# A closing norm's factor gets a place of its own, and two queries' swaps go ahead of a weight load

## The reference, cut to what matters

```python
x = first_block(x, ...)                       # ends: return _rmsnorm(x, final_norm_w)
x = second_block(x, ...)

def hybrid_layer(x, c_silu, cos, sin, norm_g, ...):
    u = rms_norm(x, norm_g) * (1 + scale) + shift
    z = u @ w_in                              # aq ak av ag iq ik iw bq bk bv bg cq ck cv cg ma mb mc
    # a: for each query the 128 best keys by an index score, attention over them
    #    score = sum over 4 heads of iw * relu(rope(iq) @ rope(ik)); top_k(score)
    # b: window attention with sinks;  c: stick-breaking attention
    merged = sigmoid(ma) * (ya @ w_br_a) + sigmoid(mb) * (yb @ w_br_b) + sigmoid(mc) * (yc @ w_br_c)
    return x + gate * (merged @ w_out)
```

## Time and profile before

| what | value |
|---|---|
| median of 3 runs | 2800.11 us (2791.91 to 2801.91) |
| the profiled execution's own time | 2794.37 us |
| its span | 2792.6 us |
| TensorE busy | 2681.3 us (96%) |
| VectorE busy | 1816.1 us (65%) |
| ScalarE busy | 1152.6 us (41%) |
| mean granted clock of TensorE | 0.981 |

### The profile page before, as it was taken

The page is one execution under the profiler, slowest core; times in us unless marked ns, Lnnn a source line. Parts: engine busy times, 40 slices in busy tenths (PEclk is TensorE's granted clock), DMA queues, the critical chain, the costliest instruction groups (busy, mean ns, idle before and its releaser), DMA issues.

```text
span 2792.6 us, 36953 instructions
## 1 busy us (share of the span) xinstructions
PE 2681.3 (96%) x14886; PEld 2154.3 (77%) x14886; DVE 1816.1 (65%) x2968; ACT 1152.6 (41%) x1900; POOL 693.0 (25%) x514
## 2 busy tenths in 40 slices
PE   6999899999999998999999999998999999999997
PEld 5877578888878676888887878776787788777776
DVE  7789668867577775877557768744546548544534
ACT  3243544323242454433224464344434455444432
POOL 0000047988700004356540032000100122000100
PEclk9999999999999998999999999999999999999999
DMA  8453034554432112344432535231223222322312
GB/s 273 122 144 104 29 121 151 166 166 159 147 119 57 59 59 83 121 143 150 139 123 85 163 94 159 85 106 33 91 64 106 85 73 80 91 76 72 96 61 78
DMA packets 281114, 302.59 MB, mean 108 GB/s; under 512 B 9968, under 2 KB 263024, under 8 KB 280944
## 3 DMA queue, kind: packets, MB, share of 16 engines
q1 hardware_dynamic: 267568, 250.21, 28.8%
q0 software_dynamic: 13088, 49.55, 5.4%
q10 hardware_dynamic: 288, 0.47, 0.1%
HBM read 289.97 MB, written 2.10 MB: 105 GB/s over the span
## 4 chain that ended last, share of the span: by engine, by line
PE 86%; DVE 7%; ACT 4%; DMA 1%; issue 1%; SPq 0%; POOL 0%; DVEq 0%; ACTq 0%
PE ps L568 84%; PE ps L776 2%; DVE wl L1410 1%; DVE hl L1416 1%; DVE adaacc L1416 1%; DMA raw<-in_w_in 1%; ACT wh L934 0%; DVE recat L1708 0%; ACT recat L934 0%; ACT hh L934 0%; DMA stage<-in_w_ada 0%; DVE rawt L1416 0%; DMA t1s<-rawt 0%; ACT att_p L934 0%; DVE ca L1416 0%
## 5 line engine op out<-in xcount | busy, mean ns | idle before, releaser
L568 PE MATMUL ps<-hh,wh 128*128 128x512 f32 x2208 | 891.8, 404 | 24.1 <-DVE wl L1410 10.2
L568 PE MATMUL ps<-hh,wl 128*128 128x512 f32 x2208 | 866.8, 393 | 0.0
L568 PE MATMUL ps<-hl,wh 128*128 128x512 f32 x2208 | 865.5, 392 | 0.0
L1410 DVE TENSOR_TENSOR wl<-raw,wh 128x2048 fp32r<-128x2048 f32 (+3 forms) x234 | 500.9, 2149 | 167.7 <-ACT wh L934 167.5
L568 PEld LDWEIGHTS ps<-hh,wh 128*128 128x128 f32 x2208 | 416.5, 189 | 140.8 <-issue 40.4
L568 PEld LDWEIGHTS ps<-hh,wl 128*128 128x128 f32 x2208 | 416.4, 189 | 92.4
L568 PEld LDWEIGHTS ps<-hl,wh 128*128 128x128 f32 x2208 | 417.3, 189 | 80.2
L934 ACT ACTIVATE wh<-raw 128x2048 fp32r<-128x2048 f32 (+3 forms) x234 | 370.0, 1591 | 205.8 <-PE ps L568 191.4
L568 PE MATMUL ps<-fh,wh 128*128 128x512 f32 x432 | 171.6, 397 | 0.0
L568 PE MATMUL ps<-fh,wl 128*128 128x512 f32 x432 | 168.3, 390 | 0.0
L568 PE MATMUL ps<-fl,wh 128*128 128x512 f32 x432 | 168.2, 389 | 0.0
(11 more groups left out here) (298 smaller groups left out, 4136.5 us busy)
## 6 DMA issues: line engine op xcount, KB each, us to landing
raw<-in_w_in SPq DMA_DIRECT2D x75, 1024.0 KB, 5.3
raw<-in_w_up SPq DMA_DIRECT2D x46, 1024.0 KB, 5.1
strewn<-in_w_ada POOLq DMA_DIRECT2D x80, 512.0 KB, 4.1
raw<-in_w_ada SPq DMA_DIRECT2D x24, 1024.0 KB, 5.3
raw<-in_w_in SPq DMA_DIRECT2D x44, 512.0 KB, 5.1
raw<-in_w_out SPq DMA_DIRECT2D x16, 1024.0 KB, 5.1
raw<-in_w_down SPq DMA_DIRECT2D x16, 1024.0 KB, 5.2
stage<-in_w_ada SPq DMA_DIRECT2D x8, 1024.0 KB, 11.6
```

Of the source, the lines that this page charges most:

```text
L568: return e.matmul(o, a, b, start=start, stop=stop, skip_group_check=True)
L1410: return e.tensor_tensor(o, a, b, op)
```

## The change

Two things. First, SyncE doesn't issue the load behind the split of the first cq chunk at once in the second stack's layers: it issues the eight swaps of iq first and the load behind them. Second, the factor of the first stack's closing norm goes to `M.fin_rr`, the last quarter of `M.bq`. The index ReLU of layer 0 then waits for the factor only, the eight scalings stand one behind each tile of the values c ("v2"), they have a cost in the planner's table, and the rotation of queries b on GpSimd waits for the last of them.

```diff
@@ Memory
         self.bq = sb("bq", [128, 4, 512])
+        self.fin_rr = self.bq[:, 3, :]
@@ COST
-    "bv": (("ACT", 0.6, True),), "bvt": (("PE", 0.5, True), ("ACT", 0.6, True)), "iw": (("PE", 0.5, True), ("DVE", 0.2, True)),
+    "final": (("DVE", 0.75, True),), "bv": (("ACT", 0.6, True),), "bvt": (("PE", 0.5, True), ("ACT", 0.6, True)), "iw": (("PE", 0.5, True), ("DVE", 0.2, True)),
@@ scalar_program, inv_rms
         if tag == ("fin", 0):
-            rr = M.nrm[:, 0, :]
+            rr = M.fin_rr
@@ scalar_program, index_scores
-        go.wait_ge(*(at("weighed", *before) if before else at("hl", ("m3", 1), KD - 1) if l else at("xf", ("m3", 0), KD - 1)))
+        go.wait_ge(*(at("weighed", *before) if before else at("hl", ("m3", 1), KD - 1) if l else at("rr", ("fin", 0))))
@@ vector_program, final
-        rr = M.nrm[:, 0, :] if w == "fin" else M.rr[:, :]
+        rr = M.fin_rr if w == "fin" else M.rr[:, :]
@@ gpsimd_program, rope
+        if nm == "bq" and l == 0:
+            go.wait_ge(*at("xf", ("m3", 0), KD - 1))
@@ sync_program
-    for kind, *rest_ in X.order:
+    for n, (kind, *rest_) in enumerate(X.order):
         if kind == "rope":
             rope(*rest_[:3])
         elif kind in ("split", "ada", "adap"):
             free.add(rest_[-1])
+        if kind == "split" and X.order[n + 1][:1] == ("em",) and X.order[n + 1][1][0] == "m3":
+            continue
+        if kind in ("split", "ada", "adap") or kind == "rope" and rest_[1:3] == ["iq", 1]:
             while loads and loads[0][1]["raw_before"] in free:
                 load(*loads.pop(0))
@@ order_block2
-    finals = [("final", ("fin", 0), "fin", k, k + 2) for k in range(0, KD, 2)] if l == 0 else []
+    finals = [("final", ("fin", 0), "fin", k, k + 1) for k in range(KD)] if l == 0 else []
@@ order_block2, main
-        if finals:
+        if finals and units[0][0] == "v2":
             mains.append(([finals.pop(0)], 1, False, None))
@@ order_block2
-    index, last = [], [("final", ("fin", 0), "fin", 6, 8)] if l == 0 else []
+    index, last = [], []
```

## The result

| | before | after |
|---|---|---|
| median of 20 runs each | 2798.22 us (2787.97 to 2806.32) | 2784.32 us (2779.76 to 2800.38) |
| the profiled execution's own time | 2794.37 us | 2782.49 us |
| its span | 2792.6 us | 2780.7 us |
| first query tile of layer 0 to that of layer 1 | 653.3 us | 643.1 us |
| from there to the end | 621.4 us | 617.1 us |

The ratio is 0.9959, 95% interval 0.995 to 0.9968: some 11 us (the two medians lie 13.9 us apart), under the bound of 0.5% that the prediction set. A later series of the same program gave 0.9969 (0.9955 to 0.9982). By the profiles layer 0 gained 10.2 us and layer 1 4.2; the first stack, which the change doesn't touch, took 2.5 us more in the execution after. Between executions it varies more than that: the first query tile starts anywhere from 1517.7 to 1531.8 us in the profiles of this study.

What follows compares the result with a forecast made beforehand. TensorE bounds the kernel (86% of the chain), so a change pays only where it waits or runs slowly. Layer 0's 9.7 plus layer 1's 1.1 us make 10.8; median forecast 2789 us, range 2776 to 2800, the forecast's own 2784 to 2795.

Steps and rivals of the forecast that it cites:

- The swaps' part, the wait removed: Second query tile: swaps ahead of the load land in 2.2 us, removing waits of 3.64 (layer 0) and 2.39 us.
- The late load: Layer 0 key tile: load issued behind eight swaps lands 5.3 us later; 1.4 us of new waiting for the residue.
- sum of 8.1 us: Whole change: estimated gain in place of 10.8 us if each load counted with 5.3 lands 0.85 us later.
- The closing factor: Layer 0 index ReLU: the 2.12 us wait goes, a new 2.5 us wait comes; layer 0 gives 9.7 us in all.
- Layer 1: Start of layer 1: only the swaps' order acts; 1.1 us stays, the rest handed on to the weights' chain.
- The planner: Layer 0 top-k steps: scalings' cost (6 us) and scores about 6 us earlier about cancel; nothing, 3 us either way.
- the rival in which the tail grows: Layer 0 attention a: scalings planned ahead of top-k steps end them later; 2801 us if the tail doubled; chance 0.11.
- my own sign of being wrong: Wrong if attention a's or b's tail changes by over 10 us, value tiles miss residues, or swaps still take 5 us.
- The cover of the scalings: Value tiles of layer 0: VectorE, busy 28.62 of 37.00 us, fits 5.5 us more, so it costs nothing.
- The load is too late: Both layers: swaps ahead give nothing as swaps stay late or weights set the pace; 2795 us; chance 0.16.
- part 1: SyncE's queue in both layers: index query swaps go ahead of the load; 3.64 us wait removed in layer 0.
- The tail goes away: Layer 0 attention a: top-k steps end a stage earlier and it spreads over matmul tiles; 2778 us; chance 0.17.

Runs made afterwards that it cites:

- e1: Kernel before with the index queries' swaps ahead of the load in both layers, nothing else; ratio to before 0.9981 (0.9968 to 0.9993).
- e4: Kernel before with the factor in its own place and the ReLU waiting for it alone; scalings and planner as before; ratio 0.9982 (0.9971 to 0.9994).
- e5: Kernel before with swaps ahead of the load and the factor in its own place; scalings unmoved, without planner cost; ratio 0.9953 (0.9938 to 0.9968).
- e2: Kernel before with the swaps ahead of the load in layer 1 only; ratio to before 0.9988 (0.9976 to 1.0).
- e12: The changed kernel unaltered, for a second profile; ratio to before 0.9969 (0.9955 to 0.9982), layer 0 645.6 us.
- e9: Changed kernel without the scalings' planner cost, two unread matmuls added before each TensorE wait in layer 0's last six attention a blocks; median 2780.77 us.

## Why the prediction was right, and where it was not

The median came to 2784.32 us where 2789 was forecast, at the lower edge of the forecast's own range of 2784 to 2795. By the profiles the two layers gave 14.4 us where 10.8 were forecast. The size is in part luck: layer 1 gave 3.1 us more than its term, two shifts of the planner met near nothing for another reason than the one given, and the clock at the start of layer 0 differs by up to 3.4 us of time (by the half) between profiles of the same start.

*The swaps' part, the wait removed.* Right: 3.64 and 2.39 us became 0.45 and none. e1 shows it alone, with 3.2 and 4.3 us. The fourth swap took 3.76 us, between the 2.2 that I took and the bound of 5.8. That the 5.76 us of before were all due to the load ahead of it was too simple: in layer 1, behind the same load, the fourth swap took 4.5 us, and the 1.25 us more of layer 0 come together with the instruction packet.

*The late load.* Right in layer 0: issue to the start of the split took 5.7 us and the key tile missed its residue by 0.89 (forecast 1.4 of new waiting here; with the 1.03 for the bank it is 1.9). The price that I set beside it from the Trainium skill (DMA: Bandwidth & Descriptors, section Bandwidth, Measured), 6.15 us for 1 MB, was too high for this load (5.70 us) and too low for the next one of layer 0 (6.58). The page's figure leaves out the time to issue, which the rows have in theirs, so the two are not quite the same thing. Its sum of 8.1 us (three loads at 0.85 us give 8.2; 8.1 also counts the load of 5.99 with 6.15) lies further from the 14.4 of the profiles than 10.8 does.

*The closing factor.* Right that the 2.12 us go, and e4 shows that the place alone does it. By e5 the scalings need not move. What did not come is the new wait of 2.5 us that I put in its stead behind the split of the next load: the second scores of layer 0 came only after 24 more matmuls, 12 more than I had counted, so the wait was covered to 0.30 us. I had carried over the order of layer 1, where the planner had written another. The same work was done 10.7 us sooner, where 9.7 were forecast, and 9.3 and 8.4 us sooner in the two other profiles of this start. So the 9.7 us are right as a size, with a wait that did not come set against clock that differs between profiles.

*Layer 1.* The mechanism was right and the term mis-sized: 4.2 us in place of 1.1. The step that failed is "load landed 2180.7, split 2182.6 and 2184.9, next load": I let the load that is held back be the one that the key tile needs. In layer 1 both buffers serve TensorE's chunks, and the load held back is one chunk further on, as the split at 2167.83 shows. The gain was not handed on. e1 and e2 gave the same 4.3 and 4.1.

*The planner.* Nothing with 3 us either way was forecast, and for the net it holds by luck: in the rest of layer 0 the changed kernel is 0.6 us worse than before by waits and clock (13.6 and half of 10.4, against 11.4 and half of 13.5), e12 2.5 us worse. But the two shifts did not cancel where I had them cancel: the rival in which the tail grows did set in (waits 7.1 to 11.8 us, length 21.7 to 32.5), and was paid for by two waits, at 1636.6 and 1649.0 in the kernel before, that I had not looked at. At 0.46 us per us of tail I would have priced the growth at 5.0 us; its waits alone came to 4.7. By my own sign of being wrong, a tail that changes by over 10 us, this step failed: measured as above it grew by 10.8. What I put at nothing because the earlier scores offset the planned cost is a loss in the tail offset by waits removed elsewhere.

*The cover of the scalings.* Right: no residue is missed at the value tiles.

*The rivals.* "The load is too late" is excluded by e1, in which part 1 alone gives 3.2 and 4.3 us, and by the 0.89 us. "The tail goes away" did not come; e9 shows what the clock's part of it would have given.

## What to carry to other kernels

Put the small transfers that an engine waits for ahead of a large load on the same queue, all of them: with four left behind the load, the last of them held an in-order engine for 3.8 us and made the load's own product late, while the two of ik, which nothing waits for, cost nothing behind it. Ask of each load held back which chunk it is and how many buffers stand before it, since one buffer more was the difference between the 1.1 us forecast and the 4.2 measured. And before a planner gets a new cost, read what the moved work had covered: here 1.4 to 4.0 us won in one place stood against 2.9 to 4.7 lost in another. And take a second profile of the same program before a gain of clock is put down to a change.

## What the hardware showed that was not expected

At the start of layer 0 removing 4.6 us of waits brought 3.4 to 6.9 us more from the clock (by the half): 13.7 us at the lower level, in two profiles of two, became 0, 3.4 and 6.8 in three profiles of the new start. The clock is not fixed by the program: its lower level in the tail took 10.4 and 17.2 us in two profiles of one program, and 24.0 in two others with the same order. Over the 20 runs of the changed kernel the mean granted clock goes from 0.985 in the shortest (2779.76 us) to 0.979 in the longest (2800.38 us). Added matmuls of 512 columns in the waits held it at 1.00 in the tail in three profiles of three. And the fourth swap of a tile, issued ahead of the load, took 3.2 to 4.0 us in layer 0 and 2.0 us in layer 1; what differs in every profile is a 16 KB packet of instructions that moves beside it.
